# Two units of weights taken together at the head of a fused two-block transformer kernel

## The reference, cut to what matters

```python
def rmsnorm(x, g):
    xf = x.astype(jnp.float32)
    y = xf * lax.rsqrt(jnp.mean(xf * xf, axis=-1, keepdims=True) + EPS)
    return (y * g.astype(jnp.float32)).astype(x.dtype)

h = rmsnorm(x, g_mix[i])
z = jnp.einsum("bsd,dn->bsn", h, w_in[i])     # 1024 -> 4608 columns
a_val, a_gt = z[..., :o1], z[..., o1:o2]      # 4 + 4 tiles of 128 columns
a = a_val * jax.nn.sigmoid(a_gt)              # goes into a 31-tap causal convolution
```

## Time and profile before

| | us |
|---|---|
| median of 3 runs (752.04 to 753.04) | 752.05 |
| the profiled execution, its own time | 752.84 |
| its span, first to last instruction | 750.8 |
| PE busy in the span | 743.0 (99%) |
| DVE, ACT, POOL busy | 578.7, 452.0, 210.6 |

### The profile page before, as it was taken

One profiled execution on the slowest core, in us unless ns is written; L12 is line 12 of the kernel. 1 busy time (PEld: TensorE's weight loads), 2 busy tenths in 40 slices (PEclk: granted clock), 3 DMA queues, 4 the chain that ended last, 5 costly groups with the idle time before them and its releaser, 6 DMA issues.

```text
span 750.8 us, 16764 instructions
## 1 busy us (share of the span) xinstructions
PE 743.0 (99%) x5950; PEld 722.7 (96%) x5950; DVE 578.7 (77%) x1049; ACT 452.0 (60%) x765; POOL 210.6 (28%) x136
## 2 busy tenths in 40 slices
PE   9999999999999999999999999999999999999997
PEld 9999999999999999999999999999999999988885
DVE  6899986877887887434987794799999999973333
ACT  7645456556665665445765798876766666643431
POOL 0477642460000000343464003322112212212220
PEclk9999999999999999999999999999999999999999
DMA  8566553565555567544444344365555555666551
GB/s 307 182 217 205 184 166 127 197 201 195 194 180 189 190 204 250 198 162 152 159 161 139 115 134 125 111 199 200 192 190 195 180 184 196 210 212 193 186 179 56
DMA packets 37917, 135.48 MB, mean 180 GB/s; under 512 B 4464, under 2 KB 4720, under 8 KB 37872
## 3 DMA queue, kind: packets, MB, share of 16 engines
q1 hardware_dynamic: 37728, 134.86, 54.4%
q10 hardware_dynamic: 144, 0.00, 0.0%
HBM read 133.80 MB, written 1.05 MB: 180 GB/s over the span
## 4 chain that ended last, share of the span: by engine, by line
PE 89%; DVE 3%; ACT 3%; issue 2%; POOL 1%; DMA 1%; SPq 0%; DVEq 0%; POOLq 0%; ACTq 0%
PE bank L1901 25%; PE bank L1902 25%; PE bank L1903 25%; PE bank L2349 4%; PE bank L2348 4%; PE bank L2347 4%; DVE w_lo L1223 1%; ACT w_hi L787 1%; DMA raw<-in_w_in 1%; POOL X L755 1%; PE bank L2176 1%; ACT score L1079 0%; PE bank L2200 0%; PE bank L1959 0%; DVE sumsq L1813 0%
## 5 line engine op out<-in xcount | busy, mean ns | idle before, releaser
L1901 PE MATMUL bank<-h_hi,w_hi 128*128 128x256 f32 x1372 | 385.9, 281 | 0.3 <-DVE w_lo L1223 0.2
L1902 PE MATMUL bank<-h_lo,w_hi 128*128 128x256 f32 x1372 | 382.9, 279 | 0.0
L1903 PE MATMUL bank<-h_hi,w_lo 128*128 128x256 f32 x1372 | 382.8, 279 | 0.0
L787 ACT ACTIVATE w_hi<-raw 128x1024 fp32r<-128x1024 f32 (+2 forms) x243 | 258.9, 1068 | 93.2 <-PE bank L1903 41.3
L1223 DVE TENSOR_TENSOR w_lo<-raw,w_hi 128x1024 fp32r<-128x1024 f32 (+2 forms) x187 | 236.6, 1268 | 85.9 <-ACT w_hi L787 84.0
L1901 PEld LDWEIGHTS bank<-h_hi,w_hi 128*128 128x128 f32 x1372 | 257.9, 188 | 1.8 <-DVE w_lo L1223 0.7
L1902 PEld LDWEIGHTS bank<-h_lo,w_hi 128*128 128x128 f32 x1372 | 258.0, 188 | 0.0
L1903 PEld LDWEIGHTS bank<-h_hi,w_lo 128*128 128x128 f32 x1372 | 257.9, 188 | 0.0
L636 POOL TENSOR_TENSOR w_lo<-raw,w_hi 128x1024 fp32r<-128x1024 f32 (+1 forms) x56 | 139.0, 2485 | 382.9 <-ACT w_hi L787 374.7
L1281 DVE TENSOR_TENSOR bank<-bank,scales 128x256 f32<-128x256 f32 x116 | 49.5, 430 | 26.3 <-PE bank L1903 17.6
L1572 DVE SCALAR_TENSOR_TENSOR cg<-bank,vec,cg 128x255 f32<-128x255 f32 x108 | 51.5, 476 | 0.7 <-ACT cg L1019 0.6
(11 more groups left out here) (235 smaller groups left out, 963.2 us busy)
## 6 DMA issues: line engine op xcount, KB each, us to landing
raw<-in_w_up SPq DMA_DIRECT2D x108, 512.0 KB, 3.3
raw<-in_w_in SPq DMA_DIRECT2D x53, 512.0 KB, 3.4
raw<-in_w_down SPq DMA_DIRECT2D x32, 512.0 KB, 4.2
raw<-in_w_down SPq DMA_DIRECT2D x16, 704.0 KB, 4.2
raw<-in_w_o SPq DMA_DIRECT2D x8, 512.0 KB, 4.3
raw<-in_w_gate SPq DMA_DIRECT2D x8, 512.0 KB, 3.4
raw<-in_w_out SPq DMA_DIRECT2D x8, 512.0 KB, 3.3
raw<-in_w_b_out SPq DMA_DIRECT2D x4, 512.0 KB, 3.6
```

The lines of the kernel that those rows point to most:

```text
L787: nc.scalar.activation(hi_of(u)[:, cols], raw[s][:, cols], ACT.Copy).then_inc(hi_ready, 1)
L1901: nc.tensor.matmul(ps, wh, hi[:, k, :], start=start and n == 0, stop=False)
L1902: nc.tensor.matmul(ps, wh, lo[:, k, :], start=False, stop=False)
L1903: last = nc.tensor.matmul(ps, wl, hi[:, k, :], start=False, stop=stop and n == len(ks) - 1)
```

## The change

Units 0 and 1 are loaded together in four pieces, each of two chunks of both units (256 KB, from a new array `w_first` laid out so), in turn with the four parts of X. ACT rounds and DVE subtracts piece by piece, across two ring slots; the last piece's low part is made unit by unit. PE multiplies each piece for unit 0 and then for unit 1. `rounded_first` is now used for unit 2, the sum over partitions stands in unit 3 behind its first two chunks, and the broadcast in unit 4 behind its first two chunks. On SP the loads of units 4 to 7 stand ahead of `vec`, `p`, `lqk` and `sinks`. ACT rounds `p` behind unit 16 rather than ahead of unit 11. The three rings become one tensor each, at the same addresses.

```diff
-        raw = [sb(f"raw{i}", [P, UNIT_MAX], past=RING_PAST) for i in range(RING)]
...
+        raw_ring = sb("raw", [P, RING, UNIT_MAX], past=RING_PAST)
...
+        raw, w_hi, w_lo = ([ring[:, s] for s in range(RING)] for ring in (raw_ring, w_hi_ring, w_lo_ring))
...
-        def first_half(half):
-            return slice(half * DC // 2 * P, (half + 1) * DC // 2 * P)
+        def piece(ring, i):
+            return ring[:, 0:2, 2 * i * P:2 * (i + 1) * P]
...
-            load_x(0)
-            load_first(0, first_in)
-            load_x(1)
-            load_first(1, raw_in[0])
-            load_x(2)
-            load_x(3)
-            load("in", 1, (1, None))
+            for i in range(4):
+                load_x(i)
+                load_first(i, first_in[i] if i < 2 else raw_in[i - 2])
             load("in", 2, (2, None))
             sp.dma_start(ident[:], d["ident"]).then_inc(ident_in, 16)
             load("in", 3, (3, None))
+            for i in range(RING, 2 * RING):
+                load("in", i, (slot(i), 1))
             sp.dma_start(vec[:], d["vec"]).then_inc(vec_in, 16)
...
-                first = RING if name in ("in", "down2") else 0
+                first = {"in": 2 * RING, "down2": RING}.get(name, 0)
...
-                if c == 1:
-                    act.wait_ge(first_in, 16)
-                    nc.scalar.activation(w_hi[0][:, first_half(0)], raw[0][:, first_half(0)], ACT.Copy
-                                         ).then_inc(first_hi, 1)
-                if c == 3:
...
-            for u in (1, 2):
-                round_unit(u)
+                if c % 2 == 1:
+                    i = c // 2
+                    act.wait_ge(first_in[i] if i < 2 else raw_in[i - 2], 16)
+                    nc.scalar.activation(piece(w_hi_ring, i), piece(raw_ring, i), ACT.Copy
+                                         ).then_inc(first_hi if i < 2 else hi_ready, 1)
+            round_unit(2)
...
             for i in range(CK):
+                if i == 2:
+                    act.wait_ge(p_in, 16)
...
+            def rest_of_first(i):
+                dve.wait_ge(first_hi if i < 2 else hi_ready, i % 2 + 1)
+                if i < 3:
+                    nc.vector.tensor_tensor(piece(w_lo_ring, i), piece(raw_ring, i),
+                                            piece(w_hi_ring, i).bitcast(f32), ALU.subtract
+                                            ).then_inc(first_lo, 1)
+                    return
+                cols = slice(6 * P, DC * P)
+                for u in range(2):
+                    nc.vector.tensor_tensor(w_lo[u][:, cols], raw[u][:, cols],
+                                            w_hi[u][:, cols].bitcast(f32), ALU.subtract
+                                            ).then_inc(lo_ready[u], 1)
...
-                if c == 1:
-                    rest_of_first(0, (first_hi, 1), first_lo)
-                if c == 3:
-                    rest_of_first(1, (hi_ready, 1), lo_ready[0])
-            for u in (1, 2):
-                rest_of_unit(u)
+                if c % 2 == 1:
+                    rest_of_first(c // 2)
+            rest_of_unit(2)
...
-            for u in range(24):
-                if u > 1:
-                    unit_here(u)
+            for i in range(4):
+                if i < 3:
+                    pe.wait_ge(first_lo, i + 1)
+                for u in range(2):
+                    if i == 3:
+                        unit_here(u)
+                    last = products(in_tile(u), u, 2 * i, (2 * i, 2 * i + 1), h2_hi, h2_lo,
+                                    i == 0, i == 3, deferred_ready("in"))
+                    if i == 3:
+                        last.then_inc(unit_done, 1)
+            pe.wait_ge(hi_ready, 3)
+            rounded_first(2)
+
+            for u in range(3, 24):
+                unit_here(u)
...
-                if u in (2, 3):
-                    first = DC - 2 if u == 2 else DC // 2
+                if u in (3, 4):
+                    first = 2
                     products(in_tile(u), slot(u), 0, range(first), hi, lo, True, False)
-                    if u == 2:
+                    if u == 3:
                         pe.wait_ge(memset_done, 3)
                         mean_squares("in")
...
+    weights["first"] = weights["in"][:2].reshape(2, P, 4, 2 * P).transpose(2, 1, 0, 3).reshape(4, P, 4 * P)
```

More of the change, by code:

```diff
@@ L320, in build @@
         UNIT_MAX = max(b for _, _, b in PHASES) * P
-        raw = [sb(f"raw{i}", [P, UNIT_MAX], past=RING_PAST) for i in range(RING)]
-        w_hi = [sb(f"w_hi{i}", [P, UNIT_MAX], f32r, past=RING_PAST) for i in range(RING)]
-        w_lo = [sb(f"w_lo{i}", [P, UNIT_MAX], f32r, past=RING_PAST) for i in range(RING)]
+        raw_ring = sb("raw", [P, RING, UNIT_MAX], past=RING_PAST)
+        w_hi_ring = sb("w_hi", [P, RING, UNIT_MAX], f32r, past=RING_PAST)
+        w_lo_ring = sb("w_lo", [P, RING, UNIT_MAX], f32r, past=RING_PAST)
+        raw, w_hi, w_lo = ([ring[:, s] for s in range(RING)] for ring in (raw_ring, w_hi_ring, w_lo_ring))
         x_at = aligned(at[0], 4 * DC * TOK)
@@ L470, in build @@
         src_ready = sem("src_ready")
-        first_in, first_hi, first_lo = sem("first_in"), sem("first_hi"), sem("first_lo")
+        first_in = [sem(f"first_in{i}") for i in range(2)]
+        first_hi, first_lo = sem("first_hi"), sem("first_lo")
         op_hi, op_lo = sem("op_hi"), sem("op_lo")
@@ L572, in load_x, with load_first @@
                              ).then_inc(x_in[n], 16)
-            def load_first(half, done):
-                sp.dma_start(raw[0][:, first_half(half)],
-                             d["w_in"][ds(0, 1)].rearrange("a p n -> (a p) n")[:, first_half(half)]
+            def load_first(i, done):
+                sp.dma_start(piece(raw_ring, i),
+                             d["w_first"][ds(i, 1)].rearrange("a p (u n) -> (a p) u n", u=2)
                              ).then_inc(done, 16)
-            load_x(0)
-            load_first(0, first_in)
-            load_x(1)
-            load_first(1, raw_in[0])
-            load_x(2)
-            load_x(3)
-            load("in", 1, (1, None))
+            for i in range(4):
+                load_x(i)
+                load_first(i, first_in[i] if i < 2 else raw_in[i - 2])
             load("in", 2, (2, None))
@@ L845, in _ @@
                 gained("in", c, g_first[:, c:c + 1])
-                if c == 1:
-                    act.wait_ge(first_in, 16)
-                    nc.scalar.activation(w_hi[0][:, first_half(0)], raw[0][:, first_half(0)], ACT.Copy
-                                         ).then_inc(first_hi, 1)
-                if c == 3:
-                    act.wait_ge(raw_in[0], 16)
-                    nc.scalar.activation(w_hi[0][:, first_half(1)], raw[0][:, first_half(1)], ACT.Copy
-                                         ).then_inc(hi_ready, 1)
-            for u in (1, 2):
-                round_unit(u)
+                if c % 2 == 1:
[4 more added lines that the diff above has]
+            round_unit(2)
             for n in range(DC // 2):
@@ L891, in round_s @@
                 nc.scalar.activation(s_hi[:, i, :], s_tile(i), ACT.Copy).then_inc(op_hi, 1)
[L893 to L896, removed]
             for i in range(CK):
+                if i == 2:
+                    act.wait_ge(p_in, 16)
+                    for c in range(2):
+                        nc.scalar.activation(p_hi[:, c, :], p_raw[:, c, :], ACT.Copy
+                                             ).then_inc(p_hi_ready, 1)
                 for r in range(3):
@@ L2033, in _ @@
                 early = u < IN_DEFERRED
-                ready = deferred_ready("in") if u == 0 else \
-                    chunk_ready("h_in") if u == IN_DEFERRED else None
+                ready = chunk_ready("h_in") if u == IN_DEFERRED else None
                 hi, lo = (h2_hi, h2_lo) if early else (h_hi, h_lo)
                 first = 0
[L2038 to L2046, removed]
-                if u in (2, 3):
-                    first = DC - 2 if u == 2 else DC // 2
+                if u in (3, 4):
+                    first = 2
                     products(in_tile(u), slot(u), 0, range(first), hi, lo, True, False)
-                    if u == 2:
+                    if u == 3:
                         pe.wait_ge(memset_done, 3)
```

## The result

The changed kernel takes 758.21 us (median of 6 runs, 756.87 to 761.19) against 752.53 for the kernel before beside it (6 runs, 752.04 to 753.86): ratio 1.0075, 95% interval 1.0062 to 1.0089, so slower by 5.7. Its profiled execution took 759.04 with a span of 756.0, against 752.84 and 750.8: the spans differ by 5.2. Of the 3.4, 0.5 is the kernel before's own median, 752.53 here and 752.05 in the forecast.

The account below looks back on a forecast made before the run. PE, busy 99% of the span, was taken as the bound, with DVE's order next. Late statistics cost 2.45 + d = 2.75 at unit 10, the rest nothing: 752.05 + 2.75 = 754.8 for the median, range 753.0 to 756.4.

Parts of the forecast that it names:

- PE from 7.18, through units 0 to 2 by 15.57: Head: PE still starts at 7.18, bound by the warm-up, and ends unit 2 at 15.57 at the soonest.
- Unit 3's low part holds PE: Before unit 3: PE wants DVE's low part at 15.57 but goes on at 16.56 + d, idle about 1.3.
- d: Delay of unit 2's landing, from pieces written in 1 KB runs: 0 to 0.54, taken as 0.3.
- The sum at 17.26 + d, the wait at unit 4, the broadcast at 21.38 + d: Units 3 and 4: sum 1.77 + d later, PE waits 0.43 for unit 4's low part, broadcast 2.88 + d later.
- Nothing is absorbed, 2.45 + d at unit 10: Unit 10: DVE's whole order moves with the broadcast, so PE begins it 2.45 + d = 2.75 later.
- Rival 1: Units 4 to 10: late statistics are absorbed, PE pays only its own two waits, 0.78 + d, so 753.1; chance 0.12.
- The rest costs nothing.: Loads of units 4 to 7 ahead of the vectors, later vectors and later rounding of `p` add no time.
- Rival 2: Load queue at the head: unit 2 lands 1.2 sooner, loss 1.55, so 753.6, or as much worse; chance 0.10.
- Rival 4: Idle before unit 3 lets PE's clock fall; one unit at the lower level costs up to 2.80, 757.6; chance 0.07.
- From there on both traces run alike, 2.7 apart.: After unit 10's first load: no further difference between the two kernels, which stay 2.7 apart.

Follow-up runs that it names:

- e11: The kernel before once more, unchanged, for a second trace: 752.30 against 752.68, ratio 0.9998.
- e9: The changed kernel once more, unchanged: 757.48 against 753.02, ratio 1.0050.
- e7: The kernel before with unit 0's two halves loaded in runs of 1 KB instead of 2 KB, same bytes: 754.44 against 753.02, ratio 1.0016.
- e5: The kernel before with only the sum over partitions moved to unit 3 and the broadcast to unit 4: 755.98 against 753.02, ratio 1.0035.
- e16: The changed kernel with four waits that are long over ahead of the warm-up: 756.86 against 752.79, ratio 1.0051.
- e17: The changed kernel with sixteen waits that are long over ahead of the warm-up: 756.20 against 752.79, ratio 1.0039.
- e4: The kernel before with only SP's new order (units 4 to 7 ahead of the vectors) and `p` rounded later: 753.58 against 752.79, ratio 1.0002.
- e3: The changed kernel with the sum between units 2 and 3 and the broadcast in unit 3 behind four chunks: 755.51 against 752.79, ratio 1.0032.
- e8: e3 with the old order on SP, vectors ahead of units 4 to 7: 753.36 against 753.02, ratio 1.0005.
- e1: The changed kernel with six unused matmuls ahead of unit 3, filling PE's idle stretch: 756.25 against 752.79, ratio 1.0037.
- e18: e17 with four unused multiplications on DVE ahead of its additions: 759.31 against 752.50, ratio 1.0092.
- e10: The changed kernel again, unchanged, for a third trace: 756.85 against 752.68, ratio 1.0050.
- e12: e7 once more, unchanged: one execution, 756.13.
- e19: e17 with the six filling matmuls of e1 before unit 3: 756.81 against 752.50, ratio 1.0047.

## Why the prediction was right, and where it fell short

- **PE from 7.18, through units 0 to 2 by 15.57.** It began at 6.64 and ended unit 2 at 15.5, having lost 0.2 and 0.3 at the second and third piece. The kernel before began at 6.12 in e11 and 7.18 in the trace shown: this start wanders by more than the gain in question.
- **Unit 3's low part holds PE.** Right. An idle stretch of 1.51 (e9: 1.33, forecast 1.3), ended by DVE's low part.
- **d.** The term that was mis-sized at the head. Taken as 0.3, "at most 0.54", it was 0.56 in the trace after (landed at 11.34 for 10.78). In the twelve traces with the pieces unit 2 landed at 10.97 to 12.08, in the middle 11.7, against 10.44 to 10.96 in the six with the old loads; d is about 0.9 against the trace that the forecast used, and 1.1 against the middle of the six, 10.6. I had priced the packets alone. A packet of 1 KB took 46 ns in the median and one of 2 KB 84, so the pieces' packets cost 64 x 46 - 32 x 84 ns = 0.26, inside the bound; the rest is delay that does not lie in the packets' own time. One part of it is visible: the issues of the pieces take SP 0.55 to 0.67 each:

```profile
L578 SPq DMA_DIRECT2D raw<-in_w_first x4: 550/551/668, 1.2 to 5.0; - x4
```

  They were 0.42 in the earlier trace rows. That the issues delay the landing by all that is missing was not separated. e7 shows that the runs, without anything else of the change, make unit 2 1.0 later.
- **The sum at 17.26 + d, the wait at unit 4, the broadcast at 21.38 + d.** Right to 0.02: with the d of each trace, the sum was due at 17.82 and stood at 17.82 (the broadcast was 1.1 later than due, by the clock); in e9 (d = 0.91) both were due at 18.17 and 22.29 and stood at 18.17 and 22.31, with a wait of 0.35 for the 0.43 forecast.
- **Nothing is absorbed, 2.45 + d at unit 10.** Right, e5 above all, and to 0.02 in e9, e16 and e17 as well (unit 10 3.37, 3.66 and 3.55 late, with a d of 0.91, 1.20 and 1.09). Rival 1 falls by DVE's 16.93 in both kernels. In the trace after PE pays in units 8, 9 and 10 by 0.54, 0.72 and 0.20, 1.46 together for the 1.6 forecast.
- **"The rest costs nothing."** True in the changed kernel, but only because DVE was late. e4 shows unit 8's load 2.8 later behind the vectors, and e3 and e8 differ by this order alone: 1.0032 and 1.0005, though their intervals overlap and unit 2 landed 0.6 later in e3.
- **Rival 2, a quicker queue.** Wrong: the loss recurs in every trace, spread differently each time. From the landing of X's first part to that of unit 2 stand nine times 256 KB, 6.0 at 0.67 each; the traces with the old loads took 0.9 to 1.4 more (the one before 1.2), the 14 with runs of 1 KB 1.4 to 2.6 more.
- **Rival 4, the clock.** Held apart from the forecast with a chance of 0.07, it came on top of it. Its reading of the warm-up holds: in e1 12 loads of the same matmul took 1.42 at a granted clock of 1.00, 0.12 each, and not 0.20. Sixteen steps at the lower level took 3.41 where 16 x 0.1165 = 1.86 would do, 1.5 more, less the 0.43 wait that they fill: 1.1. Of six traces with PE idle for 1.2 to 2.2 before unit 3, the clock fell in three (after idle stretches of 1.51, 1.33 and 2.20) and stayed up in three (1.33, 1.21 and 1.43); of the other 14 traces in none. What decides among those of 1.2 to 1.5 was not found. That the stretch is the cause rests on this count, on the mean clocks of the other executions (8 of 23 with the stretch, none of 12 with it filled), and on e18, where the longer stretch brought it back in all four. The Trainium skill, "TensorE: Matmul & The Clock Gate", Part 1, has the throttled state as the default, lifted by activity; that fits, and these traces add that the clock fell after PE had been idle for 1.33.
- **"From there on both traces run alike, 2.7 apart."** This is the step that failed: the sum put nothing after 2.45 + d, neither for the clock nor for the pace, and 0.3 for d. The traces ran 4.15 apart at unit 10, which the kernel got back by 0.5 up to 150 us (a part of it is PE's wait at 146.94 in the kernel before, which has gone), and then 1.6 further apart in stages that the change does not touch, by 1.1 ns a matmul.

The sum for the trace after: 2.45 as forecast, 0.56 for d, 1.1 for the clock, 1.6 for the pace, less the 0.5 got back: 5.2, the difference of the spans. The change itself costs 2.45 + d, and 1.1 more where the clock falls. The forecast's mechanism was right up to unit 10; two terms lay outside it, of which one was named as a rival and one was not thought of, and d was half of what it measured. This is the sum of one traced execution; for the medians of the runs the share of the pace is not shown.

What stays open: why the pace changes. Four builds are slow in all their seven traces (the changed kernel with e9 and e10, e1, e7 with e12, e19) and the others fast in all their thirteen. In e16 and e17 a few waits ahead of everything turned it, in the one traced execution of each; the medians of their runs don't follow. That this is the place of PE's instructions in memory is inferred from that, not shown. e7 kept PE's instructions and still went slow, which that account does not explain by itself. Why runs of 1 KB land later than their packets explain, and what decides whether the clock falls, stay open too. No version is clearly better than the kernel before: e8 is level with it.

## What to carry to other kernels

Before moving a small step whose result other engines wait for, follow its result to the first engine with no slack: here a sum that costs PE 0.89 wherever it stands was moved by 1.8 and its broadcast by 2.9, and 2.45 came out 20 us later. Gaps that only the start of a kernel shows are not worth opening another gap for, as the waiting time moves and an idle PE may lose its clock too. And when a trace differs in a stage that the change doesn't touch, count instructions in a stretch without waits, pad the program, and look at all executions and not at the traced one alone, before believing any difference of one or two us.

## What was not expected of the hardware

- The matmul's pace in long stretches without waits was 116.4 or 117.6 ns in the traces, the same in each repeated trace of a build, at a granted clock of 1.00: 1.6 us in 170. With four waits that were over ahead of everything, the changed kernel's trace had the faster.
- The clock fell after idle stretches of 1.33 and 1.51, in two of five such traces of up to 1.51 us; the fall began about 2 us after PE had gone on, and lasted 3.4. It cost 1.1 at unit 10 each time.
- Issuing a load of 256 KB in runs of 1 KB took 0.55 to 0.67 on SP, of 2 KB 0.42.
